# Grouped attention in two layers: weights turned three steps after their scores in place of two, and the value products one step later

## The chip, the cores and the metric

The kernel runs on one core of a Trainium2 chip. The time is device microseconds (us) of one execution on that core. Matmuls run on TensorE (PE, its weight loads PEld), reductions, products and differences on VectorE (DVE), activations and copies out of PSUM on ScalarE (ACT), some of the splitting of weights on GpSimd (POOL), and transfers are issued by SyncE (SP).

## The reference, cut to what matters

The program is one block of another kind and then two equal layers (`l` = 0, 1) on 512 tokens of width 1024. In each layer, the part that the change touches is this attention, with 8 query heads of 64, 2 key and value heads, and 512 queries against 512 keys:

```python
s = jnp.einsum('bqgrd,bkgd->bgrqk', qb, k).astype(jnp.float32) * scale
p = jax.nn.softmax(s, axis=-1).astype(v.dtype)
return jnp.einsum('bgrqk,bkgd->bqgrd', p, v)
```

Each layer has three such branches, computed from the same normed input `u`: a differential attention, a retention, and this grouped attention. Then each branch is projected, weighted by a gate and summed:

```python
projected = jnp.einsum('bsnw,nwd->bsnd', branches, w_branch[l])
gates = jax.nn.sigmoid(gate_logits.reshape(B, S, N_BRANCHES, D))
merged = jnp.sum(gates * projected, axis=2)
```

## The kernel before, in words

Everything is computed in float32 from two parts: a weight or an operand is split into a high part (`wH`, `uH`; an ACT copy, line 746) and the rest (`wL`, `uL`; a difference, on DVE at line 751 or on POOL at line 784), and a product of 128 x 512 is three sums of matmuls: high by high, high by low, low by high.

A layer has two streams of work, which are woven together by counting. The long one is the **fill**: the products of the layer's input with its weights, 64 chunks of weights per layer, each chunk's product cut into three **thirds** of eight matmuls (line 826, 2850 for the values, 1069 for the branch projections). Its chunks are, in this order: 8 tiles of queries and keys of the differential attention (`d`), 4 chunks of its values, 12 of the grouped branch's gates and projection, 8 tiles of the retention's, 4 and 4 chunks of its values and gate, 12 of the differential branch's gates and projection, and 12 of the retention branch's. The short stream is the attention itself: `gqa_steps` for the grouped attention, `diff_steps` for the differential one, `ret_steps` for the retention. These three lists of steps call `fill(n)`, which issues n thirds of the long stream between the pieces of the short one. What of the fill is left after `ret_steps` follows at its end.

In the grouped attention a **unit** u (0 to 15) is one pair of query heads p = u // 4 and one block of 128 queries. Its life is:

- `score(u)` on PE (line 3135): two score tiles of 128 x 512, in two PSUM banks.
- DVE takes each row's negative maximum (line 3233), ACT the exponential with it as a bias, into `gpr`, one of three buffers, and the row sums (line 3199). These ACT instructions release the two banks.
- DVE divides by the row sums (lines 3212 and 3215) and counts up `gw_ready`. The code of DVE does this for unit u in its step u + 1.
- `turned(u)` on PE (line 3126): the weights are transposed, four times 128 x 128 for each of the two heads, into two more banks. ACT copies them to `gwT` (line 3185).
- After four units, `value(p)` on PE (line 3161): 16 matmuls in one bank; ACT copies the result's high part (`bgH`, line 3175), DVE computes the rest (`bgL`, line 3223), and only this difference releases the bank.

PE, ACT and DVE each run through the same numbered steps, each with its own code (`gqa_pe`, `gqa_act`, `gqa_dve`). On ACT and DVE the fill's own work (copies out of PSUM, rotary products, splitting of later weights) is placed by `Follow.to(step)`: before an instruction of the attention they first do every chunk that PE has finished by then. How many these are is the table `MARKS`, which counts the thirds that `fill` has issued when a step is called, divided by three. A chunk of the `d` tiles costs ACT a scaled copy, a square, a root in two instructions, and a split (lines 3000, 3001, 924, 930, 746), and DVE three or four products (lines 3060, 3036, 3038, 3042). With it goes one more product on PE, the sums of squares (line 2917).

**Banks.** All results of the short stream and line 2917's go through four PSUM banks, `ps4` to `ps7`, handed out in turn, in the order in which `order_layer` adds them (`M.add`). A result that comes fourth after another gets its bank, and PE waits at its first matmul until that bank's reader is done. For a pair of score tiles both banks are waited for before the first matmul.

The retention ends with the mean of squares (lines 2900 and 2901 on PE), a root on ACT (a table load at line 919, then lines 924 and 930), two products on DVE (3502, 3504), and the split into `brH` (3459, ACT) and `brL` (3508, DVE). The projection of that branch, fill chunk 54 and on, reads these (line 1069). It waits for the last quarter of them at its seventh matmul.

Of the kernel before, what the change touches and what calls it, by code (L numbers as in the profile page):

```python
# [395 lines left out]
TILES = {"g": (0, 4, 1, 2, 3), "d": (0, 4, 1, 5, 2, 6, 3, 7), "r": (0, 4, 1, 5, 2, 6, 3, 7)}  # L396
def gqa_steps(score, turned, value, vturn, fill):

    for u in range(19):
        if u >= 6 and u % 4 == 2:  # L400
            value(u // 4 - 1)
        if 2 <= u < 18:
            turned(u - 2)
        fill(2 if u == 1 else 1)
        if u == 1:
            vturn()
        if u < 16:
            score(u)
        fill(1 if u < 18 else 0)
# [198 lines left out]
def build(nc, a, out, consts, attn_consts, ropes, dists, line_dram):  # L608
# [55 lines left out]
    def sem(name):  # L664
        if name not in sems:
            sems[name] = nc.alloc_semaphore(name)
        return sems[name]
# [34 lines left out]
    def M(*name, l=None, i=0, n=0):  # L702
        return Grp(orders(l)[2], "m", *name, i=i, n=n)
# [2410 lines left out]
    def gv_turn_act(st, l):  # L3114
        e = st.e
        g = M("gvt", l=l)
        o = g.take(e)
        st.w()
        g.done(st, e.activation(vv["gv"][:, :, :], o[:, :].rearrange("p (t d) -> p t d", t=NT), ACT.Copy))
        st.w()  # L3120
        e.sem_inc(sem("vv_ready"), 1)
# [43 lines left out]

    def gqa_act(st, l, follow):
        e = st.e
        for u in range(19):
            if u >= 6 and u % 4 == 2:
                p = u // 4 - 1  # L3170
                follow("gpv", p)
                g = M("gpv", p, l=l)
                o = g.take(e)
                st.w()
                st.f(e.activation(bgH[:, p, :], o[:, :], ACT.Copy), sem("bH_ready"), 27 + 20 * l + p + 1)
            if 2 <= u < 18:
                v = u - 2
                follow("gt", v)
                for m in range(2):
                    g = M("gt", v, m, l=l)  # L3180
                    o = g.take(e)
                    if v % 4 == 0 and v:
                        e.wait_ge(misc_ready, M("gpv", v // 4 - 1, l=l).nth)
                    st.w()
                    g.done(st, e.activation(gwT[:, m, :, v % 4 * P:(v % 4 + 1) * P],
                                            o[:, :].rearrange("p (k q) -> p k q", k=4), ACT.Copy))
                st.w()
                e.sem_inc(sem("gt_turned"), 1)
            if u < 16:
                follow("gs", u)  # L3190
                if u == 1:
                    gv_turn_act(st, l)
                e.wait_ge(sem("gmax_ready"), 16 * l + u + 1)
                if u >= 3:
                    e.wait_ge(misc_ready, M("gt", u - 3, 1, l=l).nth)
                st.w()
                for m in range(2):
                    g = M("gs", u, m, l=l)
                    g.done(st, e.activation(gpr[:, u % 3, m, :], g.ps[:, :], ACT.Exp, bias=gst[:, u % 3, m:m + 1],  # L3199
                                            accum_out=gst[:, u % 3, 2 + m:3 + m]))  # L3200
                st.w()
                e.sem_inc(sem("gexp_ready"), 1)

    def gqa_dve(st, l, follow):

        e = st.e
        for u in range(20):
            if 1 <= u < 17:
                v = u - 1
                e.wait_ge(sem("gexp_ready"), 16 * l + v + 1)  # L3210
                st.w()
                st.s(e.reciprocal(gst[:, v % 3, 4:6], gst[:, v % 3, 2:4]))
                st.w()
                for m in range(2):
                    st.s(e.tensor_scalar(gpr[:, v % 3, m, :], gpr[:, v % 3, m, :], gst[:, v % 3, 4 + m:5 + m], None, ALU.mult))
                st.w()
                e.sem_inc(sem("gw_ready"), 1)
            if u >= 6 and u % 4 == 2:
                p = u // 4 - 1
                g = M("gpv", p, l=l)  # L3220
                e.wait_ge(sem("bH_ready"), 27 + 20 * l + p + 1)
                st.w()
                g.done(st, e.tensor_tensor(bgL[:, p, :], g.ps[:, :], bgH[:, p, :].bitcast(F32), ALU.subtract))
                st.w()
                e.sem_inc(sem("b_ready"), 1)
            if 2 <= u < 18:
                follow("gt", u - 2)
            if u < 16:
                for m in range(2):
                    g = M("gs", u, m, l=l)  # L3230
                    o = g.take(e)
                    st.w()
                    st.s(e.tensor_reduce(gst[:, u % 3, m:m + 1], o[:, :], AX, ALU.max, negate=True))
                st.w()
                e.sem_inc(sem("gmax_ready"), 1)  # L3235
                follow("gs", u)
# [1117 lines left out]
```

## Time and profile before

| what | us |
|---|---|
| median of 3 runs | 2940.39 |
| lowest, highest | 2938.97, 2942.61 |
| the profiled execution's own time | 2939.37 |
| its span, first to last instruction | 2937.6 |
| PE busy | 2889.7 (98%) |
| DVE, ACT, POOL busy | 1834.2, 1413.2, 309.2 |

The granted clock of TensorE is 0.997 of full speed over the span. PE is the engine that sets the time, so what counts is where it is idle. In the rows below, a bracket at the end of a row holds the idle time of that engine just before the instruction, in us, and what released it.

### The profile page before, as it was taken

The page shows a single profiled execution, that of the slowest core. Times are in us where ns is not written, and L with a number is a line of the kernel's source. Part 1 is how long each engine was busy: PE and PEld are TensorE (multiplying, and loading weights), DVE is VectorE, ACT ScalarE, POOL GpSimd, SP SyncE. Part 2 cuts the span into 40 slices and gives each one's busy share as a digit, 9 for nine tenths or more (in the row PEclk, how much of TensorE's full clock was granted, in tenths as well). Part 3 has the DMA queues.
Part 4 walks back from the last instruction along what each step waited for, and adds up shares of the span by engine and source line. Part 5 has one row for each costly group of instructions (what it writes and reads, how often), then busy time and mean ns, then how long its engine had stood idle before and what let it go on. Part 6 is the DMA issues. An engine that isn't in the chain of part 4 may idle for free. (4 is left out here: it accounts for less than half of the span.)

```text
span 2937.6 us, 38352 instructions
## 1 busy us (share of the span) xinstructions
PE 2889.7 (98%) x14295; PEld 2333.4 (79%) x14295; DVE 1834.2 (62%) x2319; ACT 1413.2 (48%) x2078; POOL 309.2 (11%) x210
## 2 busy tenths in 40 slices
PE   9999999999999999999999999999999999999999
PEld 7787778888788877677777889897667777888888
DVE  4437768345854667656644787867755744587784
ACT  3556425234533446645543654445654554464442
POOL 5002300000100002211112000001221111000000
PEclk9999999999999999999999999999999999999999
DMA  7322223333323332123322433323222322433322
GB/s 193 92 72 71 60 58 94 100 94 100 107 86 104 93 98 68 48 79 87 93 72 86 124 99 101 101 82 91 56 60 72 109 72 79 122 101 101 101 87 72
DMA packets 407184, 263.44 MB, mean 90 GB/s; under 512 B 29674, under 2 KB 396124, under 8 KB 407008
## 3 DMA queue, kind: packets, MB, share of 16 engines
q1 hardware_dynamic: 401072, 250.09, 29.3%
q0 software_dynamic: 5936, 11.03, 1.3%
q8 instruction: 107, 1.75, 0.2%
q14 instruction: 69, 0.57, 0.1%
HBM read 253.70 MB, written 5.64 MB: 88 GB/s over the span
## 5 line engine op out<-in xcount | busy, mean ns | idle before, releaser
L751 DVE TENSOR_TENSOR wL<-wR,wH 128x1024 fp32r<-128x1024 f32 (+2 forms) x261 | 314.6, 1205 | 303.8 <-ACT wH L746 278.4
L826 PE MATMUL ps<-uH,wH 128*128 128x512 f32 x1184 | 483.7, 409 | 1.9 <-ACT wH L746 1.7
L826 PE MATMUL ps<-uL,wH 128*128 128x512 f32 x1184 | 463.5, 391 | 0.0
L746 ACT ACTIVATE wH<-wR 128x1024 fp32r<-128x1024 f32 (+3 forms) x352 | 361.6, 1027 | 182.1 <-DMA wR<-in_ffn_w_down_dram 54.5
L784 POOL TENSOR_TENSOR wL<-wR,wH 128x1024 fp32r<-128x1024 f32 (+1 forms) x91 | 224.7, 2470 | 1647.5 <-ACT wH L746 1647.5
L826 PE MATMUL ps<-uH,wL 128*128 128x512 f32 x1184 | 305.3, 400 | 0.0
L826 PEld LDWEIGHTS ps<-uH,wH 128*128 128x128 f32 x1184 | 223.0, 188 | 70.6 <-issue 23.3
L826 PEld LDWEIGHTS ps<-uH,wL 128*128 128x128 f32 x1184 | 219.7, 189 | 54.7 <-issue 8.9
L826 PEld LDWEIGHTS ps<-uL,wH 128*128 128x128 f32 x1184 | 223.2, 189 | 50.1 <-issue 6.5
L813 PE MATMUL ps<-uH,wH 128*128 128x512 f32 x528 | 208.3, 394 | 2.2 <-ACT wH L746 2.2
L813 PE MATMUL ps<-uL,wH 128*128 128x512 f32 x528 | 205.5, 389 | 0.0
L813 PE MATMUL ps<-uH,wL 128*128 128x512 f32 x528 | 133.0, 389 | 0.0
L813 PEld LDWEIGHTS ps<-uH,wH 128*128 128x128 f32 x528 | 99.1, 188 | 24.7 <-ACT wH L746 3.1
L813 PEld LDWEIGHTS ps<-uL,wH 128*128 128x128 f32 x528 | 99.1, 188 | 21.8 <-issue 1.4
L813 PEld LDWEIGHTS ps<-uH,wL 128*128 128x128 f32 x528 | 99.1, 188 | 20.6
L4109 DVE TENSOR_TENSOR hT<-hT,ps 128x512 f32<-128x512 f32 x128 | 88.0, 688 | 35.3 <-PE ps L3828 22.7
L3341 DVE TENSOR_REDUCE stt<-ps 128x1 f32<-128x512 f32 x64 | 44.3, 692 | 68.2 <-PE ps L3135 63.2
L1096 ACT ACTIVATE sg<-ps 128x512 f32<-128x512 f32 x48 | 28.7, 599 | 104.6 <-PE ps L826 100.6
L3199 ACT ACTIVATE gpr<-ps,stt 128x512 f32<-128x512 f32 x64 | 43.5, 684 | 70.3 <-DVEq L3235 64.4
L3277 ACT ACTIVATE dpr<-ps,stt 128x512 f32<-128x512 f32 x64 | 43.5, 685 | 67.9 <-DVEq L3343 67.7
L3828 PE MATMUL ps<-hidH,dn0H 128*128 128x512 f32 x176 | 68.7, 390 | 1.7 <-DVE hT L4109 1.7
L3828 PE MATMUL ps<-hidL,dn0H 128*128 128x512 f32 x176 | 68.6, 390 | 0.0
(590 smaller groups left out, 6385.3 us busy)
## 6 DMA issues: line engine op xcount, KB each, us to landing
wR<-in_w_in_dram SPq DMA_DIRECT2D x182, 512.0 KB, 3.8
wR<-in_ffn_w_up_dram SPq DMA_DIRECT2D x44, 512.0 KB, 3.8
wR<-in_w_mlp_in_dram SPq DMA_DIRECT2D x22, 512.0 KB, 3.7
dn0R<-in_w_mlp_out_dram SPq DMA_DIRECT2D x22, 512.0 KB
dn1R<-in_w_mlp_out_dram SPq DMA_DIRECT2D x22, 512.0 KB, 3.4
dn2R<-in_w_mlp_out_dram SPq DMA_DIRECT2D x20, 512.0 KB, 3.4
wR<-in_w_branch_dram SPq DMA_DIRECT2D x16, 512.0 KB, 3.4
wR<-in_w_out_dram SPq DMA_DIRECT2D x16, 512.0 KB, 3.9
```

The lines of the kernel that those rows point to most:

```text
L746: st.f(st.e.activation(wH[:, slot, 0:n], wR[:, slot, 0:n], ACT.Copy), hi_ready, c + 1)
L751: st.f(st.e.tensor_tensor(wL[:, slot, 0:n], wR[:, slot, 0:n], wH[:, slot, 0:n].bitcast(F32), ALU.subtract), lo_ready, c + 1 if done is Non ...
L784: e.tensor_tensor(wL[:, slot, 0:n], wR[:, slot, 0:n], wH[:, slot, 0:n].bitcast(F32), ALU.subtract).then_inc(sem("lo_pool"), 1)
L813: ins = pe.matmul(outp, w[:, k, c0:c0 + m], x[:, k0 + k, :], start=k0 == 0 and s == 0, stop=k0 + kt == kn and s == len(steps) - 1)
L826: ins = pe.matmul(o[:, :], w[:, k, :], x[:, k, :], start=s == 0, stop=s == 3 * KD - 1)
L1096: g.done(st, e.activation(sg[:, t, :], o[:, :], ACT.Tanh, bias=bias, scale=0.5))
L3199: g.done(st, e.activation(gpr[:, u % 3, m, :], g.ps[:, :], ACT.Exp, bias=gst[:, u % 3, m:m + 1], accum_out=gst[:, u % 3, 2 + m:3 + m]))
L3277: g.done(st, e.activation(dpr[:, u % 3, m, :], g.ps[:, :], ACT.Exp, bias=ast[:, u % 3, m:m + 1], accum_out=ast[:, u % 3, 2 + m:3 + m]))
L3341: st.s(e.tensor_reduce(ast[:, u % 3, m:m + 1], o[:, :], AX, ALU.max, negate=True))
L3828: ins = pe.matmul(o[:, :], w[:, k, t * P:(t + 1) * P], h[:, k, :], start=s == 0, stop=s == 11)
L4109: to.done(st, e.tensor_tensor(hT[:, j, :], hT[:, j, :], o[:, :], ALU.add))
```

## The change

On all three engines the grouped attention gets a twentieth step. A unit's weights are turned in step u + 3 (before: u + 2), and the value product of a head pair is issued in steps 7, 11, 15 and 19 (before: 6, 10, 14 and 18). The scores, the maxima, the exponentials and the division by the sums stay in their steps.

```diff
@@ -396,11 +396,11 @@
 def gqa_steps(score, turned, value, vturn, fill):
 
-    for u in range(19):
-        if u >= 6 and u % 4 == 2:
+    for u in range(20):
+        if u >= 7 and u % 4 == 3:
             value(u // 4 - 1)
-        if 2 <= u < 18:
-            turned(u - 2)
+        if 3 <= u < 19:
+            turned(u - 3)
         fill(2 if u == 1 else 1)
         if u == 1:
             vturn()
@@ -3165,16 +3165,16 @@
     def gqa_act(st, l, follow):
         e = st.e
-        for u in range(19):
-            if u >= 6 and u % 4 == 2:
+        for u in range(20):
+            if u >= 7 and u % 4 == 3:
                 p = u // 4 - 1
                 follow("gpv", p)
...
-            if 2 <= u < 18:
-                v = u - 2
+            if 3 <= u < 19:
+                v = u - 3
                 follow("gt", v)
@@ -3215,7 +3215,7 @@
-            if u >= 6 and u % 4 == 2:
+            if u >= 7 and u % 4 == 3:
                 p = u // 4 - 1
                 g = M("gpv", p, l=l)
@@ -3223,8 +3223,8 @@
-            if 2 <= u < 18:
-                follow("gt", u - 2)
+            if 3 <= u < 19:
+                follow("gt", u - 3)
```

Three things move with it: the order in which the four banks are handed out, the place of the fill's chunks among ACT's and DVE's instructions, and, since the grouped attention now takes 39 thirds of the fill where it took 38, everything in the differential attention and the retention, which stands one third later in the fill.

ACT, layer 0, around the first value product, before (`gpr`: exponentials of one unit; `bgH`: the value product's copy; `gwT`: the turned weights' copies; `raw` to `wH`: one chunk of the `d` tiles):

```order
L3199 ACTIVATE gpr,stt<-ps,stt 128x512 x2
L3175 ACTIVATE bgH<-ps 128x512
L3185 ACTIVATE gwT<-ps 128x4x128 x2
L3199 ACTIVATE gpr,stt<-ps,stt 128x512 x2
L3000 ACTIVATE raw<-ps,lp 128x512
L3001 ACTIVATE sq<-ps 128x512
L924 ACTIVATE rs<-ps,cn 128x512
L930 ACTIVATE rs<-rs 128x512
L746 ACTIVATE wH<-wR 128x1024
```

The same place in the changed kernel:

```order
L3199 ACTIVATE gpr,stt<-ps,stt 128x512 x2
L3000 ACTIVATE raw<-ps,lp 128x512
L3001 ACTIVATE sq<-ps 128x512
L924 ACTIVATE rs<-ps,cn 128x512
L930 ACTIVATE rs<-rs 128x512
L746 ACTIVATE wH<-wR 128x1024
L3175 ACTIVATE bgH<-ps 128x512
L3185 ACTIVATE gwT<-ps 128x4x128 x2
```

The chunk, which came after the value product's copy, now stands ahead of it. At the second value product it is the other way round: before, a chunk stood ahead of the copy, and now none does. At the third and fourth none does in either kernel.

PE, layer 0, steps 9 and 10, with the banks, before (L3135: scores of unit 9; L2917: sums of squares; L3161: second value product; L3126: turned weights of unit 8):

```order
L3135 MATMUL ps7<-qk_g_154 128x256
L3135 MATMUL ps4<-qk_g_154 128x256
L3135 MATMUL ps7<-qk_g_154 128x256
L3135 MATMUL ps4<-qk_g_154 128x256
L826 MATMUL ps0<-uH_50,wL_53 128x512 x8
L2917 MATMUL ps5<-sq_151,cn_60 128x512
L3161 MATMUL ps6<-gwT_171,vv_g_160 64x512 x8
L3126 MATMUL ps7<-cn_60,gpr_170 128x128 x4
L3126 MATMUL ps4<-cn_60,gpr_170 128x128 x4
```

The same place in the changed kernel (L3126: unit 7):

```order
L3135 MATMUL ps5<-qk_g_154 128x256
L3135 MATMUL ps6<-qk_g_154 128x256
L3135 MATMUL ps5<-qk_g_154 128x256
L3135 MATMUL ps6<-qk_g_154 128x256
L826 MATMUL ps0<-uH_50,wL_53 128x512 x8
L2917 MATMUL ps7<-sq_151,cn_60 128x512
L3126 MATMUL ps4<-cn_60,gpr_170 128x128 x4
L3126 MATMUL ps5<-cn_60,gpr_170 128x128 x4
```

In both, turned weights go into a bank that the scores of unit 9 have just used (`ps7` and `ps4` before, `ps5` now, by the second head's). Before, the value product stands between them; now nothing does but line 826 and line 2917.

ACT, layer 0, last head of the retention, before (L3449 to L3451: copies of its output; L919 to L930: the root; L3459: the split):

```order
L3449 ACTIVATE nrmt<-ps 128x512
L3450 ACTIVATE rqH<-ps 128x512
L3451 ACTIVATE ro<-ps 128x512
L919 ACT_TABLE_LOAD
L924 ACTIVATE nrmt<-ps,cn 128x512
L930 ACTIVATE nrmt<-nrmt 128x512
L3459 ACTIVATE brH<-ro 128x512
L1096 ACT_TABLE_LOAD
```

The same place in the changed kernel:

```order
L3449 ACTIVATE nrmt<-ps 128x512
L3450 ACTIVATE rqH<-ps 128x512
L3451 ACTIVATE ro<-ps 128x512
L1096 ACTIVATE sg<-ps 128x512
L746 ACTIVATE wH<-wR 128x1024
L919 ACT_TABLE_LOAD
L924 ACTIVATE nrmt<-ps,cn 128x512
L930 ACTIVATE nrmt<-nrmt 128x512
L3459 ACTIVATE brH<-ro 128x512
L1096 ACT_TABLE_LOAD
```

A gate and a split of the fill (fill chunk 52) now stand ahead of the root. The orders of POOL and SP are the same in both kernels.

## Rows read from the trace of the kernel before

**Rows 1.** Windows: us; busy PE, PEld, DVE, ACT, POOL; clock, DMA share, GB/s.

```profile
1141.30:1267.40 126.10, 120.28 (x613) 83.69 (x612) 81.20 (x118) 80.20 (x150) 29.21 (x12) 1.00 0.19 52
1267.40:1430.00 162.60, 162.60 (x762) 121.29 (x762) 107.29 (x157) 83.82 (x143) 30.36 (x14) 1.00 0.31 89
1430.00:1564.00 134.00, 134.00 (x527) 98.28 (x526) 60.36 (x78) 60.53 (x82) 22.79 (x10) 1.00 0.26 77
2057.50:2183.60 126.10, 120.31 (x613) 83.69 (x612) 81.36 (x118) 80.24 (x150) 28.98 (x12) 1.00 0.19 52
```

**Rows 2.** Timeline of PE, grouped attention, layer 0: start, us, instruction [idle before].

```profile
1167.14 0.66 PE L3126 MATMUL ps<-cn,gpr 128*128 128x128 f32 x4 [1.40 <-ACT gpr L3199]
1170.04 1.14 PE L3135 MATMUL ps<-qk_g 64*128 64x256 f32 x8 [0.40 <-ACT rs L924]
...
1179.82 3.65 PE L3161 MATMUL ps<-gwT,vv_g 128*64 128x512 f32 x16
...
1186.81 1.13 PE L3135 MATMUL ps<-qk_g 64*128 64x256 f32 x8 [0.46 <-DVE bgL L3223]
...
1208.97 1.02 PE L2917 MATMUL ps<-sq,cn 128*128 128x512 f32 x2
1209.92 3.65 PE L3161 MATMUL ps<-gwT,vv_g 128*64 128x512 f32 x16
...
1218.00 1.13 PE L3135 MATMUL ps<-qk_g 64*128 64x256 f32 x8 [1.56 <-DVE bgL L3223]
...
1224.39 1.10 PE L2917 MATMUL ps<-sq,cn 128*128 128x512 f32 x2 [0.49 <-ACT gpr L3199]
1225.76 1.13 PE L3135 MATMUL ps<-qk_g 64*128 64x256 f32 x8 [0.28 <-ACT gwT L3185]
...
1232.01 1.13 PE L3135 MATMUL ps<-qk_g 64*128 64x256 f32 x8 [0.37 <-ACT gpr L3199]
...
1235.88 0.60 PE L3126 MATMUL ps<-cn,gpr 128*128 128x128 f32 x4
1237.32 0.66 PE L3126 MATMUL ps<-cn,gpr 128*128 128x128 f32 x4 [0.84 <-ACT gpr L3199]
```

**Rows 3.** Timeline of DVE, grouped attention, layer 0.

```profile
1163.70 0.88 DVE L3215 TENSOR_SCALAR gpr<-gpr,stt 128x512 f32<-128x512 f32 x2
...
1181.05 2.74 DVE L3038 TENSOR_TENSOR qk_d<-qk_d,partner 128x512 f32<-128x512 f32 x1
1183.91 0.69 DVE L3042 TENSOR_TENSOR qk_d<-qk_d,rs 128x512 f32<-128x512 f32 x1
...
1209.43 1.49 DVE L3233 TENSOR_REDUCE stt<-ps 128x1 f32<-128x512 f32 x2
```

**Rows 4.** Timeline of ACT, grouped attention, layer 0.

```profile
1211.01 0.69 ACT L3199 ACTIVATE gpr<-ps,stt 128x512 f32<-128x512 f32 x1 [4.09 <-DVEq L3235]
...
1215.38 1.06 ACT L746 ACTIVATE wH<-wR 128x1024 fp32r<-128x1024 f32 x1
1216.54 0.60 ACT L3175 ACTIVATE bgH<-ps 128x512 fp32r<-128x512 f32 x1
```

**Rows 5.** Timelines of ACT, then PE, then DVE, end of the retention, layer 0.

```profile
1564.88 1.28 ACT L919 ACT_TABLE_LOAD   x1 [2.59 <-PE ps L2901]
...
1571.20 0.60 ACT L1096 ACTIVATE sg<-ps 128x512 f32<-128x512 f32 x1
...
1564.16 0.39 PE L2900 MATMUL ps<-rqH,onesR 128*128 128x512 f32 x1
...
1570.06 1.98 PE L826 MATMUL ps<-uH,wL 128*128 128x512 f32 x8
1571.87 0.39 PE L1069 MATMUL ps<-brH,wH 128*128 128x512 f32 x1
...
1569.84 0.69 DVE L3508 TENSOR_TENSOR brL<-ro,brH 128x512 fp32r<-128x512 f32 x1 [0.76 <-ACT brH L3459]
```

**Rows 6.** Timeline of POOL, grouped attention, layer 0.

```profile
1180.82 2.43 POOL L784 TENSOR_TENSOR wL<-wR,wH 128x1024 fp32r<-128x1024 f32 x1 [6.37 <-ACT wH L746]
```

## Prediction, made before the changed kernel was run

> **What bounds the kernel now.** I read first the windows of busy time, cut at the places where the attention's three parts begin. PE is busy for 120.28 of 126.10 us in the grouped attention of layer 0 and for 120.31 in that of layer 1, and for all of the time in the windows of the differential attention and the retention behind it, at a granted clock of 1.00 [rows 1]. So PE's stream sets the time; there are 5.8 us per layer that it stands still, all in the part that is changed, and none behind it. DVE is busy for 81 and ACT for 80 of the 126 us [rows 1]: neither is full, but a result that is late on them is what PE waits for.
>
> Next I read PE's own timeline in that window, for every idle time and its releaser. There are eight: 1.40, 0.40, 0.46, 1.56, 0.49, 0.28, 0.37 and 0.84, in sum 5.80 us [rows 2]. Layer 1 has the same eight. The reader should ask of each what the instruction waits for, its input or its bank. The change moves `turned(v)` a step away from the division that makes its input. But no wait is for that. The tightest case is unit 2: DVE's division begins at 1163.70 and takes 0.88, so it is over at 1164.58 [rows 3], and PE turns that unit's first head without a wait and stops only at 1165.74 (1167.14 less 1.40), in front of the second head, 1.2 us after the divisions of both. The second head waits for an ACT exponential, that of unit 3, because it goes into the bank that unit 3's scores leave. The 0.84 at 1237.32 is the same case: the first head's turn runs at 1235.88, the second's is held [rows 2]. The waits of 0.46 and 1.56 stand before scores that take the bank of a value product in their own step; the other four (0.40, 0.49, 0.28, 0.37) are banks too.
>
> So the waits belong to the order in which four banks go round, and to ACT's queue, not to the distance that the change widens.
>
> The Trainium skill says in "Perfetto Trace Analysis", Identifying Performance Opportunities, that the same gap repeating on the engine that should be saturated can mean too few buffers in SBUF or PSUM. The trace agrees: eight gaps, all for a bank. By that rule an extra step of delay, which adds no bank, would bring nothing.
>
> **The change, part by part.** It adds and removes no product: PE has the same matmuls, DVE and ACT the same work, POOL and SP the same order. The costs are therefore new waits less old ones.
>
> *Turning later.* The input had slack already, so the extra step returns 0 directly. PE has one turn less behind it in steps 2 to 18, but DVE and ACT are started by the scores and shift along with PE, so this cancels. The same banks follow each other in steps 3 to 5: step 4 turns unit 1 in place of unit 2, and its second head again gets the bank of unit 3's first scores. So 1.40 and the 0.40 behind it stay.
>
> *First value product (step 7, was 6).* Before, ACT copied it at once, at a cost to PE of 0.46. Now a chunk of the `d` tiles stands ahead of that copy. That is how the second value product stood before, so I carry its row over if the start is the same. There the exponentials start at 1211.01, 1.09 after the value product at 1209.92; ACT then needs until 1216.54 to start the copy, and the score waits 1.56 [rows 2, 4]. Now: PE, at 1179.82, does a turn (about 0.9), eight matmuls (1.9), scores (1.1), eight matmuls (1.9) and sums of squares (0.95, from 1208.97 to 1209.92) first, so the value product starts at about 1186.6 [rows 2]. DVE ends line 3042 at 1184.60, then divides (1.2 with its reciprocal) and takes the maxima (1.49), which gives exponentials at about 1187.6 [rows 3], 1.0 after the value product. The same start, so the same wait: 1.56 in place of 0.46. What followed it follows again, since DVE's chunk now stands between the difference and the next maxima: 0.49, 0.28 and, one step on, 0.37, in steps 8 and 9.
>
> *Step 10.* It had the value product ahead of the turn. Now the turn of unit 7 comes with no cover, and its second head takes the bank of unit 9's scores. The two rows of this kind show 1.40 (step 4, DVE on time) and 0.84 (step 13, after a wait of 0.37 that had held PE back) [rows 2]. Step 9 now has that 0.37, so I take 0.84. A chunk of the `d` tiles is still behind it, so the 0.40 of step 4 returns too, as a score waits for the bank of line 2917.
>
> *Second value product (step 11, was 10).* No chunk ahead of its copy, and eight matmuls and a turn between it and the score: 0 in place of 1.56. But it now reads a copy of turned weights that ACT makes in the step before, behind a chunk. I count 0.1 for that; 0 to 0.4 are the ends, 0.4 being the largest wait in the rows for a result just behind such a chunk.
>
> *Step 13.* A second head takes the bank of unit 12's scores, as before. But step 12 has no wait ahead of it now, so I take the row of the undelayed case, 1.40, not 0.84; these are the ends.
>
> *Third and fourth value products (steps 15 and 19).* No wait before and none now: ACT has a light load there. The last copy of turned weights now stands behind a chunk; PE has eight matmuls between. 0, with 0.4 as the upper end.
>
> Sum of one grouped attention: 1.40 + 0.40 + 1.56 + 0.49 + 0.28 + 0.37 + 0.84 + 0.40 + 0.1 + 1.40 = 7.24, less 5.80, is +1.4 us. Two layers: +2.9.
>
> *One third later in the fill.* In the differential attention each step has three or four thirds, about 8 us, and PE waits for nothing there [rows 1]. Chunks that change their place by one cost ACT 1.7 to 4 us in front of one copy, which that fits in: 0. At the end of the retention it is tighter. PE's last mean of squares is at 1564.16; `brL` is done at 1570.53 (1569.84 plus 0.69), and PE needs it at the seventh matmul of line 1069, at 1571.87 plus 6 times 0.226, or 1573.2: slack 2.7 [rows 5]. Now eight matmuls fewer lie between, 1.8 us (1570.06 to 1571.87), so it is needed at 1571.4. And a gate (0.60) and a split (1.06) stand ahead of the root on ACT. ACT's table load started at 1564.88; with the gate starting at about 1564.4, once its product is done, it starts at 1566.1 or 1566.2, some 1.3 later [rows 4, 5]. `brL` is then done at 1571.8, 0.4 too late, and 0.1 for the signal: 0.5 per layer, 1.0 for both. The ends are 0 (the cover holds) and 1.5 (the split waits for its transfer, as some do).
>
> Total: 2.9 + 1.0 = +3.9 us on the profiled execution's own 2939.37, which is 2943.3. The median of the runs lies 1.0 above that execution, so 2944.3 is the time that I name.
>
> **The rivals.** A measurement of this kernel can tell about 0.2%, or 5.9 us, from no change; all that I forecast lies inside.
>
> *A. The forecast.* New bank waits and a late `brL`, +2 to +5.5 us. Chance 0.5.
>
> *B. No net change.* The waits change their places but not their sum: the order of the banks is turned by one step against a pattern of three steps per two chunks, so what one value product gains the other loses, and the retention's cover holds. 2940.4, give or take 1.5. For it: the eight gaps are there because ACT and DVE lag behind in the first thirteen steps, and their work is the same. Against it: the second value product was both the worst and the one that now gets free, and the first takes over exactly its row, so a full step 10 is left over as a new gap. Chance 0.25.
>
> *C. Faster.* If the waits on the exponentials (1.40, 0.49, 0.37, 0.84, in sum 3.10 per layer) were in truth for late weights, the extra step would take all of them: 2940.4 less 6.2 is 2934.2. For it: the releaser named is `gpr`, the tile that is turned. Against it: line 3199 is the exponential, not the division, and the first heads are not held. Chance 0.09.
>
> *D. Slower by more, through DVE and POOL.* A DVE product with two inputs from SBUF takes 2.74 us at 1181.05 where its like takes 0.69; POOL's split ran from 1180.82 to 1183.25, and DVE's ended 0.5 after it [rows 3, 6]. So DVE stood still for 2.05. Reordered chunks can put one more such meeting ahead of the maxima in steps 7 to 13, where lateness goes straight to PE. The point from which it decides is DVE's product starting within POOL's 2.4 us. If two more per layer are hit, with 0.2 to 0.5 of slack used up first, that is 2 x 1.8 us per layer: 3.9 + 7.2, or about 2951.5; one per layer gives 2948. Chance 0.16.
>
> The Trainium skill, "SBUF — State Buffer", Who interferes with whom, states the rule: a DVE instruction with two SBUF inputs contends with a GpSimd instruction that reads SBUF, one with a single such input outside the 2-port modes does not. The trace agrees for the row at 1181.05. The maxima, which read PSUM, keep their 1.49.
>
> **How the numbers follow.** Cases inside 0.2% are A, B and a part of D: 0.73 in all. Faster by more than that: C without its weak end, 0.08. Slower by more: most of D and the upper end of A, 0.19. The time is A's, 2944.3; A's own range is 2942.5 to 2946.5. The range for 8 in 10 takes in B's lower end and D's milder case: 2938.5 to 2948.5.
>
> **What the changed profile would show.** Right: PE idle for about 7.2 us in each grouped attention where it was 5.8; a score behind the first value product that waits about 1.5 for `bgL`, none behind the second; a second head's turn that waits at step 10, where there was no gap; the gap of 1.40 at step 4 unchanged; and one new wait of line 1069 at the retention's end, with ACT's gate and split ahead of the load at line 919. Wrong: the gap at step 4 gone (then the weights were late, C); DVE products of 2.7 us at new places ahead of maxima (D); or new waits in the differential attention, where I count none.

## The result: 10 us slower, and the profile after

| kernel | median us | lowest, highest | runs |
|---|---|---|---|
| before | 2940.68 | 2938.78, 2942.61 | 8 |
| after | 2950.53 | 2949.84, 2951.82 | 8 |

The ratio of after to before is 1.0033, 95% interval 1.0023 to 1.0044. The changed kernel is 9.85 us slower. The prediction named 2944.3 with a range of 2938.5 to 2948.5, and gave "slower by over 0.2%" a chance of 0.19: it was wrong.

The windows of the trace after, with cuts at the first scores of the grouped attention, the first of the differential attention and the first of the retention, then the same grouped attention in layer 1 (columns as in [rows 1]):

```profile
1143.00:1279.50 136.50, 127.91 (x645) 87.76 (x644) 82.03 (x119) 83.11 (x153) 31.86 (x14) 1.00 0.19 51
1279.50:1451.80 172.30, 171.30 (x793) 128.74 (x793) 105.57 (x162) 85.43 (x149) 27.68 (x12) 1.00 0.32 92
1451.80:1564.00 112.20, 112.20 (x443) 82.90 (x442) 51.50 (x69) 53.11 (x70) 21.50 (x9) 1.00 0.24 71
2063.60:2200.10 136.50, 127.94 (x645) 87.74 (x644) 82.33 (x119) 82.76 (x153) 31.80 (x14) 1.00 0.19 51
```

The same cuts in the trace before:

```profile
1141.30:1273.10 131.80, 125.98 (x639) 86.18 (x638) 81.90 (x119) 81.92 (x152) 32.14 (x14) 1.00 0.19 53
1273.10:1443.80 170.70, 170.70 (x793) 128.88 (x793) 110.02 (x159) 87.16 (x149) 28.35 (x12) 1.00 0.31 90
2057.60:2189.30 131.70, 125.91 (x637) 86.18 (x636) 81.95 (x119) 81.90 (x152) 31.81 (x14) 1.00 0.20 53
```

The grouped attention takes 4.7 to 4.8 us more per layer; 1.8 of this is a third of the fill (eight matmuls, 0.226 us from start to start) that is now done inside it, so 2.9 are lost. The differential attention has the same number of PE instructions (793) and takes 1.6 us longer, with 1.0 of PE's time idle, where before there was none. Both layers show it alike. The clock is 1.00 in all of them.

PE's own timeline says which instructions wait. Layer 0 of after, grouped attention (start, us, instruction, in brackets the idle time ahead and its releaser):

```profile
1167.93 0.66 PE L3126 MATMUL ps<-cn,gpr 128*128 128x128 f32 x4 [1.65 <-ACT gpr L3199]
1170.83 1.13 PE L3135 MATMUL ps<-qk_g 64*128 64x256 f32 x8 [0.40 <-ACT rs L924]
...
1187.31 3.65 PE L3161 MATMUL ps<-gwT,vv_g 128*64 128x512 f32 x16
...
1195.36 1.13 PE L3135 MATMUL ps<-qk_g 64*128 64x256 f32 x8 [1.53 <-DVE bgL L3223]
...
1201.75 1.10 PE L2917 MATMUL ps<-sq,cn 128*128 128x512 f32 x2 [0.51 <-ACT gpr L3199]
1203.12 1.14 PE L3135 MATMUL ps<-qk_g 64*128 64x256 f32 x8 [0.28 <-ACT gwT L3185]
...
1209.37 1.13 PE L3135 MATMUL ps<-qk_g 64*128 64x256 f32 x8 [0.34 <-ACT gpr L3199]
...
1214.68 0.65 PE L3126 MATMUL ps<-cn,gpr 128*128 128x128 f32 x4 [0.85 <-ACT gpr L3199]
...
1217.58 1.13 PE L3135 MATMUL ps<-qk_g 64*128 64x256 f32 x8 [0.40 <-ACT rs L924]
...
1239.70 0.65 PE L3126 MATMUL ps<-cn,gpr 128*128 128x128 f32 x4 [1.34 <-ACT gpr L3199]
...
1249.29 1.13 PE L3135 MATMUL ps<-qk_g 64*128 64x256 f32 x8 [1.28 <-ACT gpr L3199]
...
1426.02 0.51 PE L2850 MATMUL ps<-wH,uH 128*128 128x512 f32 x1 [0.36 <-ACT raw_r L3003]
...
1449.48 0.47 PE L826 MATMUL ps<-uH,wH 128*128 128x512 f32 x1 [0.64 <-ACT vv_r L2870]
...
1579.90 0.50 PE L1069 MATMUL ps<-brH,wH 128*128 128x512 f32 x1 [0.34 <-DVEq L3510]
```

These answer to [rows 2], and the brackets of the attention add up to 8.58 us where they were 5.80. Nine of its ten waits were forecast, to within 0.25 us each (the 0.25 is step 4: 1.65 for 1.40). One was not: 1.28 in front of the scores of step 14. Of the last three, which stand behind the attention, only that of line 1069 was forecast.

What holds the scores of step 14 is ACT's exponential of unit 13, which stands late because DVE's maxima of unit 13 are. DVE, the same stretch:

```profile
1240.58 0.88 DVE L3215 TENSOR_SCALAR gpr<-gpr,stt 128x512 f32<-128x512 f32 x2
1241.61 0.69 DVE L3036 TENSOR_TENSOR partner<-partner,cs_d 128x512 f32<-128x512 f32 x1
1242.34 0.69 DVE L3038 TENSOR_TENSOR qk_d<-qk_d,partner 128x512 f32<-128x512 f32 x1
1243.14 2.82 DVE L3042 TENSOR_TENSOR qk_d<-qk_d,rs 128x512 f32<-128x512 f32 x1
1246.11 1.49 DVE L3233 TENSOR_REDUCE stt<-ps 128x1 f32<-128x512 f32 x2
```

POOL in that stretch:

```profile
1243.03 2.39 POOL L784 TENSOR_TENSOR wL<-wR,wH 128x1024 fp32r<-128x1024 f32 x1 [9.19 <-ACT wH L746]
```

The last rotary product starts 0.11 us after POOL's split, takes 2.82 in place of 0.69, and ends 0.54 after it. The maxima cannot start before, and the exponential follows at 1247.69. The same place in before, rows of POOL, DVE, PE and ACT:

```profile
1240.66 2.39 POOL L784 TENSOR_TENSOR wL<-wR,wH 128x1024 fp32r<-128x1024 f32 x1 [7.67 <-ACT wH L746]
1240.77 2.83 DVE L3042 TENSOR_TENSOR qk_d<-qk_d,rs 128x512 f32<-128x512 f32 x1
1242.85 3.65 PE L3161 MATMUL ps<-gwT,vv_g 128*64 128x512 f32 x16
1245.32 0.69 ACT L3199 ACTIVATE gpr<-ps,stt 128x512 f32<-128x512 f32 x1 [3.35 <-DVEq L3235]
```

So the hold is not new. The exponential came 5.57 us after its scores there (1239.75 to 1245.32) and comes 5.56 after them now (1242.13 to 1247.69). But before, the value product of the third pair, 3.65 us of matmuls, stood between the scores of units 13 and 14 and covered the delay; now it comes a step later, and PE waits.

### The profile page after: what moved, and what is told of

The parts are those of the page before. It is cut to its first block and busy times, and to the rows that moved or that the text cites. A ratio compares the mean times of both kernels' runs of the same rounds, so it can differ in the third digit from the quotient of the medians.

```text
span 2948.8 us, 38358 instructions
## 1 busy us (share of the span) xinstructions
PE 2894.3 (98%) x14295; PEld 2335.9 (79%) x14295; DVE 1824.6 (62%) x2319; ACT 1410.3 (48%) x2076; POOL 306.7 (10%) x210
```

## The experiments

Fourteen kernels ran. Each stands beside runs of the kernel before on the same chip (medians of 2940.4 to 2941.3 in the four groups: e1 to e4, e5 to e8, e9 to e11, e12 to e14), and the ratios are against those. Differences from after are against its 2950.53, which was not run again beside them. "Waits" are PE's brackets in layer 0's grouped attention; layer 1 agrees within 0.1 us, but for e9 to e11 (9.82, 10.46 and 8.15 there).

| run | median us | ratio to before, 95% interval | waits in the attention |
|---|---|---|---|
| e1 after, no third in step 19 | 2946.82 | 1.0021, 1.0012 to 1.0029 | 8.54 |
| e2 before, one third more | 2943.53 | 1.0008, 0.9999 to 1.0017 | 5.77 |
| e3 after, copies first | 2944.92 | 1.0015, 1.0007 to 1.0024 | 6.49 |
| e4 before, copies first | 2936.57 | 0.9984, 0.9975 to 0.9993 | 3.66 |
| e5 after, POOL only writes | 2921.04 | 0.9932, 0.9918 to 0.9946 | 0.29 |
| e6 before, POOL only writes | 2919.64 | 0.9927, 0.9914 to 0.9941 | 0.28 |
| e7 after, e1 and e3 together | 2941.91 | 1.0004, 0.9995 to 1.0013 | 6.39 |
| e8 after, one third in step 1 | 2942.40 | 1.0007, 0.9997 to 1.0016 | 7.02 |
| e9 before, splits on DVE | 2955.99 | 1.0051, 1.0038 to 1.0065 | 9.33 |
| e10 after, splits on DVE | 2956.22 | 1.0053, 1.0039 to 1.0066 | 9.09 |
| e11 e9 and copies first | 2956.63 | 1.0054, 1.0041 to 1.0068 | 9.73 |
| e12 before, POOL in halves | 2936.71 | 0.9986, 0.9977 to 0.9995 | 4.78 |
| e13 after, POOL in halves | 2943.52 | 1.0009, 1.0000 to 1.0018 | 6.24 |
| e14 e4 and e12 together | 2933.13 | 0.9973, 0.9963 to 0.9983 | 3.03 |

### The third that moved: e1 and e2

e1 is after without the first fill of step 19; e2 is before with the second fill issued in its last step too.

```diff
# e1, on after
-        fill(2 if u == 1 else 1)
+        fill(2 if u == 1 else 1 if u < 19 else 0)
# e2, on before
-        fill(1 if u < 18 else 0)
+        fill(1)
```

> The changed kernel, but its last step issues no third of the fill, so that the grouped attention takes 38 thirds as before and everything behind it stands where it stood before the change. Theory: the change costs 10 us in two parts, bank waits in the grouped attention (its gaps sum to 8.6 us per layer against 5.8) and three waits behind it that come from the shift by one third (line 2850 0.36, line 826 0.64, line 1069 0.34; counted from start to start 2.1 us per layer). Then this kernel loses the second part, 4.3 us: 2946.2, with those three gaps gone and the gaps in the grouped attention unchanged. Rival: the whole loss comes from the grouped attention, and a stall taken away behind it comes back at another place: 2950.5.

> The kernel before with one third of the fill more in its grouped attention (in step 18), and nothing else changed. Theory (two parts): the three waits behind the grouped attention appear by this alone, +4.3 us: 2945.0; gaps in the grouped attention stay at 5.8 us per layer. Rival (all in the grouped attention): no change, 2940.7.

e1 gave 2946.82, 3.7 less than after. Its differential attention:

```profile
1276.80:1447.50 170.70, 170.70 (x794) 128.88 (x793) 110.69 (x160) 87.74 (x150) 28.91 (x13) 1.00 0.32 90
```

The same stretch in e2:

```profile
1277.30:1449.60 172.30, 171.31 (x794) 128.75 (x794) 105.60 (x162) 85.35 (x148) 27.67 (x12) 1.00 0.32 89
```

One third more makes the two waits (170.7 becomes 172.3) in a kernel without the change, and taking it away removes them from the kernel with it. The wait of 0.34 at line 1069 comes and goes with them. e2's time is 2.9 us above before (1.5 less than was expected), but its interval reaches down to 0.9999, so the stretch is the proof rather than the time. In the trace after, the three start-to-start distances are 0.76, 1.03 and 0.73 where such matmuls follow each other at 0.23: 0.53, 0.80 and 0.50, together 1.8 us per layer, where the brackets say 1.34. The next matmul comes another 0.08 to 0.11 late each time, which makes 2.1.

The traces show a reason why both came out under the 4.3 us of the theory. Further on in layer 0 two waits get shorter with the added third. They are those of lines 3828 and 954, which are 1.85 and 1.61 in before and 1.84 and 1.58 in e1, but 1.49 and 1.14 in after and 1.50 and 1.09 in e2. That gives some 0.8 us back.

### The copy that stands behind a chunk: e3 and e4

ACT does the fill's chunks up to the place that `follow` names. Without that call the value product's copy goes ahead of the chunk of its own step. In e4 the fourth keeps the call.

```diff
# e3, on after; e4, on before, keeps it for p == 3
-                follow("gpv", p)
```

> The changed kernel, but ACT copies each value product before it does the chunk of the fill that now stands ahead of it (line 3171 left out); the chunk follows behind that copy. Theory: the gap of 1.53 before the scores of step 7 is ACT's queue, and the 0.51, 0.28 and 0.34 behind it follow from it; all four go, 2.7 us per layer: 2945.1. Rival: DVE sets the pace in these steps (it has the same work), so the lateness turns up one or two units later at another bank, and the time stays within 1.5 us of 2950.5.

> The kernel before, with the same edit for the first three value products (line 3171 kept only for the fourth, where ACT must free the banks of the values first). The second value product, in step 10, had a chunk ahead of its copy. Theory (ACT's queue holds the bank): the gaps 1.56, 0.49, 0.28 and 0.37 go, 2.7 us per layer: 2935.3. Rival (DVE sets the pace): within 1.5 us of 2940.7, with the lateness at another bank.

Both fell, e3 as expected and e4 by somewhat less: 2944.92, which is 5.6 less than after, and 2936.57, which is 4.0 less than its before (5.4 had been expected of each). e3's ACT at the first value product:

```profile
1188.30 0.69 ACT L3198 ACTIVATE gpr<-ps,stt 128x512 f32<-128x512 f32 x1 [3.88 <-DVEq L3234]
...
1190.92 0.60 ACT L3174 ACTIVATE bgH<-ps 128x512 fp32r<-128x512 f32 x1 [1.17 <-PE ps L3161]
1191.64 0.69 ACT L3000 ACTIVATE raw<-ps,lp 128x512 f32<-128x512 f32 x1
```

The same place in after, with the chunk ahead:

```profile
1188.37 0.69 ACT L3199 ACTIVATE gpr<-ps,stt 128x512 f32<-128x512 f32 x1 [3.87 <-DVEq L3235]
...
1192.73 1.06 ACT L746 ACTIVATE wH<-wR 128x1024 fp32r<-128x1024 f32 x1
1193.89 0.60 ACT L3175 ACTIVATE bgH<-ps 128x512 fp32r<-128x512 f32 x1
```

The copy starts 3.0 us earlier, and the waits of 1.53, 0.51, 0.28 and 0.34 are gone. Not all of it is won: in step 10, where the wait was 0.85, it is now 1.43, since nothing has held PE back. The wait for a late exponential is only moved by what PE lost before it. The edit frees 2.5 us of the attention in after (1143.07 to the last value product's second row at 1276.96, which is 133.89; in e3 131.38) and 2.6 in before (129.16 to 126.56). So this cost is not one that the change brought; it only changed which value product pays it.

What e3 has and e4 has not are, for the most part, waits at the two places from which a value product went away: in step 10 the second head's turn and the scores behind it wait 1.43 and 0.39, and in step 14 the scores wait 1.28. In return e4's 0.46 behind the first value product is gone.

The distance between e3 and e4 is 8.4 us, nearly as large as between the two kernels: the copies explain little of it.

### The added third and the copies together: e7

> The kernel after with both edits of the earlier runs: no third in step 19, and the value copies of ScalarE ahead of the split of the chunk beside them. Theory (the added third behind and the order of the copies are two separate costs): 2950.5 - 3.7 - 5.6 = 2941.2, with 6.5 us of waits per layer in the grouped attention and none behind it. Rival (the copies and the third share one cost): 2944 or more, with waits left in the differential attention or at the retention's start.

2941.91. The two costs add up, and this version of after can't be told from before (interval 0.9995 to 1.0013). PE waits nowhere behind the attention. What remains against e4, 5.3 us, is the delay of the turns and the value products alone.

### Which third stands where: e8

```diff
# on after
-        fill(2 if u == 1 else 1)
+        fill(1)
```

> The kernel after, with one third in place of two at the first fill of step 1: 38 thirds as before, each later third falls one place later against the scores. Theory (waits follow from which third stands beside a value copy and beside a late exponential): none behind the attention (-4), the wait of step 7 (1.53) gone because no chunk's split stands ahead of that copy, a new one of up to 1.7 us ahead of scores 1, whose cover it was: 2944 to 2948. Rival (the delay of three steps itself costs, whatever the thirds): 2946.8, as with no third in step 19, and 8.5 us of waits per layer.

2942.40, below the band of the theory, and 4.4 us below e1, which has as many thirds in the attention. The new wait ahead of scores 1 is there (1.58), and the 1.5 for the value product's difference is gone, both as expected. The wait of 1.28 at step 14 is gone as well, which I had not counted; the value product of the last pair waits 0.63 for the turned weights instead. So with a delay of three steps the attention costs only 0.9 us per layer more than before (130.08 against 129.16) when the thirds stand one place later, and 2.9 when they do not. The rival, that the delay costs the same whatever the thirds, is refuted. Why it is cheaper is only in part shown: e8 also has fewer products of DVE that POOL holds up, six in each grouped attention where before and after have eight.

### POOL beside DVE: e5 and e6

```diff
# line 784, on after and on before
-        e.tensor_tensor(wL[:, slot, 0:n], wR[:, slot, 0:n], wH[:, slot, 0:n].bitcast(F32), ALU.subtract)
+        e.memset(wL[:, slot, 0:n].bitcast(F32), 0.0)
```

> The kernel after, in which POOL's split of a chunk of weights only writes its result (zeros) and reads nothing: the low part of the weights that POOL splits is left out of the products. Theory (late scores come from VectorE's rope operations of 2.7 to 2.8 us that stand behind POOL's split, where they take 0.69 undisturbed): VectorE's long operations fall to 0.69 us, and TensorE's waits of step 4 (1.65 + 0.40), of step 10 (0.85 + 0.40), of step 13 (1.34) and of step 14 (1.28) go or shrink to under 0.5 each, some 5 of the 8.6 us per layer: about 2940. Rival (these waits come from the chain exponentials, weights and transposes alone, and VectorE has slack): TensorE's waits stay within 0.5 us of 8.6 per layer and the time within 2 us of 2950.5.

> The kernel before with the same edit (POOL's split only writes; the low part of those weights is left out). Theory: of 5.8 us of waits per layer those of step 4 (1.40 + 0.40) and step 10 (0.84) go: about 2935, and the distance between after and before falls from 10 us to about 5, since the wait of step 14 and one part of step 13's hang on POOL. Rival: nothing moves, 2940.6, and the distance stays 10.

These two kernels leave out of the products the low part of the weights that POOL splits. This moved the time most: 2921.04 and 2919.64, 29 and 21 us less, about three and four times what was expected. Not all of it is in this attention. There the traces show 9.6 us less per layer in e5 and 6.6 in e6 (the lengths are given below), and the first scores come 9.0 and 5.8 us earlier, so the rest was gained in the block ahead. That start moves by itself too: the eight kernels before, after, e1 to e4, e7 and e8, whose order up to there is the same, have it between 1141.4 and 1144.9.

DVE in e5, one rotary chunk while POOL writes from 1150.23 to 1151.18:

```profile
1149.84 0.69 DVE L3060 TENSOR_TENSOR qk_d<-raw,cs_d 128x512 f32<-128x512 f32 x1
1150.64 0.69 DVE L3036 TENSOR_TENSOR partner<-partner,cs_d 128x512 f32<-128x512 f32 x1
1151.36 0.69 DVE L3038 TENSOR_TENSOR qk_d<-qk_d,partner 128x512 f32<-128x512 f32 x1
1152.16 0.69 DVE L3042 TENSOR_TENSOR qk_d<-qk_d,rs 128x512 f32<-128x512 f32 x1
```

PE then waits 0.29 us in the whole attention in after and 0.28 in before, so the other waits of both kernels, those for banks and for ACT's copies too, hung on what POOL's splits did to DVE or on how long they took. Here the attention takes 124.25 us in after and 122.52 in before, measured as above, and the difference of 1.73 is the third that moved in: the delay costs nothing. Behind it, line 2850 no longer waits, lines 826 and 1069 still do (0.64 and 0.34).

The Trainium skill, "SBUF — State Buffer", Who interferes with whom, says that a DVE instruction with two SBUF inputs contends with a GpSimd instruction that reads SBUF, not with one that only writes. The runs agree on both halves: 2.82 beside the split of 2.39, 0.69 beside the write of 0.95.

The edit changed two things, the reads and the length of POOL's instruction; e12 and e13 keep the reads and change the length.

### POOL's split in two halves: e12, e13 and e14

```diff
# line 784; e14 has e4's edit too
+        h = n // 2
-        e.tensor_tensor(wL[:, slot, 0:n], wR[:, slot, 0:n], wH[:, slot, 0:n].bitcast(F32), ALU.subtract).then_inc(...)
+        e.tensor_tensor(wL[:, slot, 0:h], wR[:, slot, 0:h], wH[:, slot, 0:h].bitcast(F32), ALU.subtract)
+        e.tensor_tensor(wL[:, slot, h:n], wR[:, slot, h:n], wH[:, slot, h:n].bitcast(F32), ALU.subtract).then_inc(...)
```

> The kernel before with POOL's split of a chunk in two instructions of half its columns each; the same reads and writes in all. Theory (an operation of VectorE that POOL holds up goes on when POOL's current instruction ends): VectorE's operations of 2.7 us beside POOL shrink to at most 1.3 + 0.7 = 2.0, the waits of steps 4 and 10 fall by 0.7 to 1.3 each, and the time to about 2930, half of what POOL only writing gave. Rival (POOL keeps what it holds from one instruction to the next): stretches of 2.7 us and 2940.6 as before.

> The kernel after with the same edit. Theory: the waits of steps 4, 10, 13 and 14 each fall by 0.7 to 1.3, the time to about 2936, and the distance to before narrows from 10 to about 6. Rival: 2950.5, and the distance of 10 stays.

> The kernel before with POOL's split in two halves and the first three value copies ahead of the split of the chunk beside them. Theory: the two gains stand on different waits, so 2936.6 - 10 = about 2927. Rival: 2936.6, where POOL keeps what it holds.

DVE in e12, a rotary chunk:

```profile
1155.81 0.69 DVE L3062 TENSOR_TENSOR qk_d<-raw,cs_d 128x512 f32<-128x512 f32 x1
1156.61 1.61 DVE L3038 TENSOR_TENSOR partner<-partner,cs_d 128x512 f32<-128x512 f32 x1
1158.25 1.66 DVE L3040 TENSOR_TENSOR qk_d<-qk_d,partner 128x512 f32<-128x512 f32 x1
1160.02 0.69 DVE L3044 TENSOR_TENSOR qk_d<-qk_d,rs 128x512 f32<-128x512 f32 x1
```

POOL in e12, its two halves:

```profile
1156.38 1.29 POOL L785 TENSOR_TENSOR wL<-wR,wH 128x512 fp32r<-128x512 f32 x1 [4.96 <-ACT wH L746]
1157.63 1.74 POOL L786 TENSOR_TENSOR wL<-wR,wH 128x512 fp32r<-128x512 f32 x1
```

DVE's product ends 0.55 after POOL's first half; POOL's second half is the one that is held then (1.74 against 1.29), and DVE's next product ends 0.54 after it. Here the two took turns, instruction by instruction. The rival, that POOL keeps what it holds, is refuted. What the chunk costs DVE only falls from about 2.1 (2.82 less 0.69 in after) to 1.9 us (0.92 and 0.97) here, since both halves meet a product. Where only one does, it is halved, and that is the case ahead of step 14. DVE in e13:

```profile
1241.24 1.73 DVE L3044 TENSOR_TENSOR qk_d<-qk_d,rs 128x512 f32<-128x512 f32 x1
1243.11 1.49 DVE L3235 TENSOR_REDUCE stt<-ps 128x1 f32<-128x512 f32 x2
```

2.82 became 1.73. The wait of the scores of step 14, on PE in e13:

```profile
1246.29 0.49 PE L3137 MATMUL ps<-qk_g 64*128 64x256 f32 x2 [0.16 <-ACT gpr L3201]
```

1.28 became 0.16: this wait hangs on the length of one POOL instruction. The times fell less than expected, since the chunk that both halves meet gains little (step 4: 1.65 to 1.19): 2943.52 for 2936, 2936.71 for 2930. The distance between the two kernels narrowed to 6.8 us.

e14 gave 2933.13, ratio 0.9973 (0.9963 to 0.9983), better than both kernels by 7.5 us and more; 2927 had been expected, but the two gains did add up (4.0 for the copies' order and 4.6 for the halves, in sum 8.6; measured 8.2). The Trainium skill, "Perfetto Trace Analysis", Optimizing Scalar/DVE Operations, suggests breaking up instructions of ScalarE or VectorE where these are not saturated but make other engines wait. It says so of those two engines only; e12 shows the same for POOL, which is 10% busy: 4.6 us for one line.

### The splits on DVE: e9, e10 and e11

```diff
# on before (e9), after (e10), and e4 (e11)
-BESIDE |= {_o[0].names[_name] for _o in ORDERS[1:] for _name in _o[0].names if _name[0] in ("d", "dv") and _name != ("d", 0)}
...
-    place = (x - FIRST) % LAYER_CHUNKS
-    return place % 2 == (0 if place < len(TILES["g"]) else 1)
+    return False
```

> The kernel before with the splits of the layers' weights that POOL did (91 chunks less the few of the first block) done by VectorE, at the place its other splits have. VectorE's time from 1141 to 1269 us was 81.5 with POOL's reads beside it and 67.4 with POOL only writing, so POOL's reads cost it 14.1 there; 13 splits of 1.23 us are 16.0. Theory (the late scores come from when VectorE is held up, and a split on VectorE is a shorter hold than the 2.0 us behind POOL, at a fixed place after the rope operation): waits per layer fall from 5.8 to about 3, and the time to about 2934. Rival (only VectorE's sum counts): no change, 2940 to 2943.

> The kernel after with the same edit. Theory: as with POOL only writing, the distance between after and before falls from 10 us to some 2 to 4 (the three short waits behind the attention remain, 1.3 us in brackets per layer): 2937. Rival (the delay of three steps costs by itself): the distance stays near 10, about 2945 to 2950.

> The kernel before with both: all splits of the layers' weights on VectorE, and the first three value copies of ScalarE ahead of the split of the chunk beside them (which alone gave 2936.6). Theory (two separate costs): 2936.6 less what the run beside this one gains over 2940.6, so about 2930. Rival (the copies' order matters only while scores are late anyway): no better than 2934.

A miss: about 2956 for all three, 15 us slower than before. In e9 DVE has no stretched product, but it waits at a new place:

```profile
1172.26 0.69 DVE L3058 TENSOR_TENSOR qk_d<-raw,cs_d 128x512 f32<-128x512 f32 x1 [0.26 <-ACTq L3003]
1174.93 1.22 DVE L749 TENSOR_TENSOR wL<-wR,wH 128x1024 fp32r<-128x1024 f32 x1 [1.98 <-ACT wH L744]
1176.27 0.69 DVE L3034 TENSOR_TENSOR partner<-partner,cs_d 128x512 f32<-128x512 f32 x1
```

It stands still 1.98 us for ACT's high part, with the rest of the rotary chunk and the next maxima behind, so the hold is 3.2 us (1.98 and 1.22) where POOL's was 2.1. PE's waits grew to 9.33 us, two of them 2.12 and 1.92 long, and the granted clock fell, which of all runs only e9 to e11 show in the attention. Windows of e9:

```profile
1160.00:1180.00 20.00, 17.84 (x94) 13.07 (x90) 14.13 (x22) 11.38 (x21) 0.00 (x0) 1.00 0.20 56
1180.00:1200.00 20.00, 18.87 (x86) 11.27 (x86) 11.39 (x21) 13.11 (x26) 0.00 (x0) 0.91 0.20 57
1200.00:1220.00 20.00, 18.08 (x85) 12.34 (x84) 13.35 (x21) 11.39 (x21) 0.00 (x0) 0.91 0.12 34
1220.00:1240.00 20.00, 18.07 (x94) 11.77 (x94) 10.43 (x18) 12.90 (x23) 0.00 (x0) 1.00 0.20 58
```

The granted clock of 0.91 is a mean of the two levels, 2.4 GHz for most of the window and 1.2 GHz for a part; the two long waits end at 1181.13 and 1207.76, in these two windows, and the low clock stands right behind them (0.50 from 1182 to 1184, 0.57 from 1208 to 1212). Nine hundredths of 40 us are 3.6 us. With the longer waits (9.33 less 5.80 is 3.5) that makes the 7.1 us by which the attention grew (136.31 against 129.16). That before and after come out alike here tells nothing of the change: both are governed by the new wait. The edit does not test what I meant it to, since it moved the work and also put a wait in front of it.

## Why the prediction was wrong

**What bounds the kernel: right.** PE's stream sets the time, and the gaps are waits for banks. Rival C, late weights, is refuted by the first of them: with one step more the wait at step 4 did not go but was 1.65.

**Steps 7 to 13: right.** The first value product took over the row of the second to 0.03 us (1.53 for 1.56, with the exponentials 1.06 after it where 1.0 was worked out), followed by 0.51, 0.28 and 0.34. Step 10 gave 0.85 and 0.40 where 0.84 and 0.40 stood, step 13 1.34 for 1.40, step 11 none for 0.1.

**Third and fourth value products: this step failed.** "No wait before and none now: ACT has a light load there." I asked only whether a value product would be late. The change also takes the third one out from between the scores of units 13 and 14, where it was the cover for a late exponential: 1.28 per layer. For that I would have had to ask, at each place that a value product leaves, what now follows what, and whose bank it takes. No wait stood there in the trace of before, but the hold did, 2.83 us at 1240.77, with the value product beside it as its cover. With POOL's hold cut in half this wait is 0.16, and with the thirds one place later it is gone.

**One third later in the fill: this step failed too.** For the differential attention I wrote 0, on the ground that what a moved chunk costs ACT in front of one copy fits into the 8 us of a step. It did not at two places, and they cost 1.6 us per layer (170.7 became 172.3). Line 2850 took a bank that ACT had to clear with the copy at 3003, which stood behind an exponential (0.36), and the retention's first third stood behind the values' copy of line 2870, which ACT made after three copies of the last value product (0.64). That no wait stood there before, with PE at 100%, said nothing about how much slack there was. The end of the retention, which I did work out (0.5 per layer), came out at 0.50 start to start, 0.6 with the matmul behind it.

**The sizes: brackets were too small.** A wait costs PE more than its bracket. In the rows behind the attention a matmul of 0.39 us starts 0.23 after the one before it, so the two overlap by 0.16, and a bracket counts only from the end of the last one. The first matmul behind a wait takes 0.47 to 0.51, and the next starts 0.31 to 0.34 after it. So three brackets of 1.34 in sum cost 2.1 us per layer.

**Rival D: its time came out, its mechanism did not.** The time lies within D's 2948 to 2951.5, and that is luck. D spoke of new meetings of DVE with POOL in steps 7 to 13. There are no more than before: in each grouped attention eight products of DVE are stretched in both traces (1.41 to 2.84 us), in layer 0 by 14.5 us in sum before and 14.4 after. What D had right is what a hold ahead of the maxima does to PE. The one that now costs 1.28 in step 14 was there before; it lost its cover. Of the 2.1 us per layer behind the attention D says nothing; only the wait of line 2850 hangs on POOL too, by e5.

The sum by the traces: 2.9 us per layer in the attention (1.4 forecast), 1.6 in the differential attention up to the retention's start (0 forecast) and 0.6 at its end (0.5 forecast) make 5.1, twice that 10.2. Layer 0 gets 0.8 back at lines 3828 and 954, which leaves 9.4. From the first scores to the last instruction the two traces differ by 9.5 (1805.7 and 1796.2), the medians by 9.85. The profiled executions differ by 11.2, because the one of after was 1.7 us later at the first scores already; the order is the same up to there and that start moves by more than this between kernels that share it, so it is no part of the change.

What stays open: how much of the 2.9 each of the two moves (the turn and the value product) costs by itself was not tried. With one buffer of turned weights the value product must be issued before the next pair's first turn, so neither can be delayed by a step alone.

## What to carry to other kernels

When an instruction is moved, the place that it leaves is a change as well: list what it stood between, and ask which late result it was covering. A stretch without waits has unknown slack, and a stream that shifts by one piece has to be followed through all of it, bank by bank. And before the order is tuned, look for operations of VectorE that now and then take several times their usual time beside GpSimd: here 5.5 of 5.8 us of waits per layer went when GpSimd only wrote, and cutting its instruction in two gave 4.6 us.

## What the runs showed of the hardware

- In e12 DVE's products and POOL's halves took turns, instruction by instruction: DVE took 1.61, then POOL 1.74 for 1.29, then DVE 1.66 for 0.69. With POOL's instruction cut in two a single hold was shorter (1.73 for 2.82 ahead of step 14), but where both halves met a product two were held.
- A `memset` of 128 x 1024 on POOL (0.95 us) did not stretch a DVE product with two SBUF inputs (0.69).
- The granted clock was 1.00 in the attention of after, with waits of up to 1.65 us, and 0.91 over the two 20 us windows of e9 in which PE waited 2.12 and 1.92 us. A wait of 2.12 did not always do it: in e11 one ended at 1179.23, and the window from 1180 to 1200 stayed at 1.00.
- DVE's total time did not show the problem: 81.5 us in the 128 us from 1141 in before, 82.15 in e9, whose kernel takes 15 us more, 75.58 in e12, whose kernel takes 5 less. Before and after have the same 14.5 us of holds per grouped attention, within 0.2, and differ in what stands beside them.
